# Last feed-forward network of a two-layer encoder: 18 of its 22 gate/up tile pairs as seven block products of 256 tokens, in place of eight

## What is computed

```python
D_MODEL, SEQ, D_FF = 1024, 512, 2816

def swiglu(h, w_gu, w_down):
    g, u = jnp.split(h @ w_gu, 2, axis=-1)
    return (jax.nn.silu(g) * u) @ w_down

# end of each layer i
h = modulate(rms_norm(x), sh3, sc3)
x = x + 0.5 * g3[:, None, :] * swiglu(h, ffn2_w_gu[i], ffn2_w_down[i])
x = rms_norm(x, post_gain[i])
```

## Time and profile before

| | before |
|---|---|
| median of 3 executions | 1981.63 us (1981.16 to 1982.28) |
| span of the profiled execution, first to last instruction | 1979.4 us |
| TensorE busy | 1951.1 us, 99% |
| VectorE busy | 1142.1 us, 58% |
| ScalarE busy | 720.1 us, 36% |
| GpSimd busy | 212.1 us, 11% |
| TensorE on the chain that ended last | 94% of the span |
| data moved by DMA | 263.97 MB, mean 133 GB/s |

### The profile page before, as it was taken

One profiled execution on the slowest core, in us unless ns is written; L12 is line 12 of the kernel. 1 busy time (PEld: TensorE's weight loads), 2 busy tenths in 40 slices (PEclk: granted clock), 3 DMA queues, 4 the chain that ended last, 5 costly groups with the idle time before them and its releaser, 6 DMA issues.

```text
span 1979.4 us, 23447 instructions
## 1 busy us (share of the span) xinstructions
PE 1951.1 (99%) x9060; PEld 1620.7 (82%) x9060; DVE 1142.1 (58%) x1720; ACT 720.1 (36%) x1068; POOL 212.1 (11%) x245
## 2 busy tenths in 40 slices
PE   6999999999999999999999999999999999999998
PEld 5888888888888888888888888878888888888887
DVE  7665564799857655645864453586554573333335
ACT  5222222464743213224422221356565452223134
POOL 3110000017701100100110000001101000000000
PEclk9999999999999999999999999999999999999999
DMA  8665552322126655622564443233322233222322
GB/s 336 227 215 172 197 191 96 106 89 86 33 64 223 204 185 183 235 81 89 172 200 138 165 155 116 91 101 113 96 86 86 62 103 106 103 88 94 97 80 69
DMA packets 76350, 263.97 MB, mean 133 GB/s; under 512 B 8897, under 2 KB 11073, under 8 KB 76274
## 3 DMA queue, kind: packets, MB, share of 16 engines
q1 hardware_dynamic: 55296, 190.34, 29.0%
q0 software_dynamic: 20256, 72.02, 11.1%
q10 hardware_dynamic: 722, 0.61, 0.1%
HBM read 260.66 MB, written 2.13 MB: 133 GB/s over the span
## 4 chain that ended last, share of the span: by engine, by line
PE 94%; DVE 3%; POOL 1%; issue 1%; DMA 0%; ACT 0%; SPq 0%; DVEq 0%; ACTq 0%; POOLq 0%
PE bank L1495 30%; PE bank L1500 29%; PE bank L1496 29%; PE bank L1943 1%; DVE dve_tmp L1068 1%; PE bank L1960 1%; PE bank L1875 1%; PE bank L1719 1%; DVE h_lo L1059 1%; PE bank L1721 1%; PE bank L1720 1%; PE bank L1932 0%; PE bank L1850 0%; DVE wlo L871 0%; POOL rstd L389 0%
## 5 line engine op out<-in xcount | busy, mean ns | idle before, releaser
L1495 PE MATMUL bank<-h_hi,whi 128*128 128x512 f32 x1808 | 711.3, 393 | 5.4 <-ACT h_hi L553 2.8
L1496 PE MATMUL bank<-h_hi,wlo 128*128 128x512 f32 x1808 | 705.1, 390 | 0.0
L1500 PE MATMUL bank<-h_lo,whi 128*128 128x512 f32 x1808 | 593.6, 390 | 2.4 <-POOL h_lo L405 2.4
L507 ACT ACTIVATE whi<-wraw 128x1024 fp32r<-128x1024 f32 x338 | 347.0, 1053 | 267.4 <-PE bank L1500 263.9
L871 DVE TENSOR_TENSOR wlo<-wraw,whi 128x1024 fp32r<-128x1024 f32 x324 | 388.9, 1223 | 60.1 <-ACT whi L507 59.8
L1495 PEld LDWEIGHTS bank<-h_hi,whi 128*128 128x128 f32 x1808 | 340.5, 188 | 78.9 <-issue 7.3
L1500 PEld LDWEIGHTS bank<-h_lo,whi 128*128 128x128 f32 x1808 | 339.7, 188 | 75.1 <-POOL h_lo L405 2.9
L1496 PEld LDWEIGHTS bank<-h_hi,wlo 128*128 128x128 f32 x1808 | 340.6, 188 | 68.7
L1495 PE MATMUL bank<-hid_hi,whi 128*128 128x512 f32 (+1 forms) x856 | 328.7, 384 | 0.0
L1500 PE MATMUL bank<-hid_lo,whi 128*128 128x512 f32 (+1 forms) x856 | 328.0, 383 | 0.0
L1496 PE MATMUL bank<-hid_hi,wlo 128*128 128x512 f32 (+1 forms) x856 | 327.9, 383 | 0.0
(11 more groups left out here) (256 smaller groups left out, 1359.5 us busy)
## 6 DMA issues: line engine op xcount, KB each, us to landing
wraw<-in_w_units_dram SPq DMA_DIRECT2D x306, 512.0 KB, 3.5
arena<-in_mod_t_dram POOLq DMA_DIRECT2D x96, 512.0 KB, 5.0
mod_tile<-in_mod_t_dram POOLq DMA_DIRECT2D x32, 512.0 KB, 4.9
wraw<-in_w_units_dram SPq DMA_DIRECT2D x32, 384.0 KB, 3.5
arena<-in_mod_t_dram SPq DMA_DIRECT2D x12, 512.0 KB, 9.6
arena<-in_w_units_dram SPq DMA_DIRECT2D x10, 512.0 KB, 4.5
xT<-in_xt_dram SPq DMA_DIRECT2D x8, 256.0 KB, 4.3
sq<-k_roots POOLq DMA_DIRECT2D x8, 256.0 KB, 3.6
```

The costliest lines, as they stand in the source:

```text
L507: act.activation(whi[:, s % RING, :, :], wraw[:, s % RING, :, :], ACT.Copy).then_inc(hi_ready, 1)
L1495: pe.matmul(dst, whi[:, w, k, :], hi_, start=first, stop=False)
L1496: pe.matmul(dst, wlo[:, w, k, :], hi_, start=False, stop=False)
L1500: return pe.matmul(dst, whi[:, s % RING, k, :], lo_, start=False, stop=last)
```

## The change

In FFN 3, pairs 4 to 7 of the first third and every pair of the other two are computed in another way (`SUM_PAIRS`, 18 pairs). The 128 x 1024 gate weights, the 128 x 1024 up weights and the 1024 x 512 input make a 2 x 2 by 2 x 2 block product: rows gate and up, K in halves `low_k` and `high_k`, tokens in halves `first` and `second`. Done block by block that is eight products (each of 4 K tiles, 128 rows, 256 tokens). The change does it with seven products of sums of blocks (the scheme of Strassen and Winograd) and adds the results. A block product is 12 matmuls of 256 tokens; a pair is 84 of them.

What that adds and moves:

- Once, before the first such pair, GpSimd makes `hsum = h_hi + h_lo` (8 instructions, `sum_h`) and four sums of its blocks of 128 x 1024 (`combine_h`). ACT rounds these (`round_t`) and DVE splits them (`split_t`). The fourth overwrites a part of `h_hi` and `h_lo`, so it waits for the last plain pair.
- For each such pair GpSimd makes four sums of weight blocks of 128 x 512 (`combine_w`).
- ACT and DVE split seven parts of 128 x 512 per pair (`part_hi`, `part_lo`) in place of two units of 128 x 1024. There is room in `whi` and `wlo` for the parts of one pair only, so part p of the next pair may be written when product p of this one is done (`part_free`).
- For each pair ACT copies two results of 256 tokens out of PSUM (`x_keep`, `z_keep`) and takes silu in two halves; DVE makes five sums of 256 tokens (`u2`, `u3`, two halves of `ups`, and the second half of `act_tmp`) and the product of 512, now with both inputs in SBUF. TensorE has a wait inside the pair ahead of five of the seven products.
- `hid_lo` of these pairs, "the remainder of the gated product", is made by GpSimd (`hid_rest`) and not by DVE.
- The buffers of the attention stage (`qk`, `pt_hi`, `pt_lo`, `v_hi`, `v_lo`) become slices of one tensor, `mix`, in which the split sums of `h` lie. The loops over pairs in FFN 3 are written out, not run as hardware loops. The name `job` now maps a unit to its number in the semaphore counts.

```diff
+SUM_FFN = (3,)
+PLAIN_PAIRS = 4
+SUM_PAIRS = [third_units(f, t)[0] + 2 * n for f in SUM_FFN for t in range(3)
+             for n in range(0 if t else PLAIN_PAIRS, THIRDS[t][1])]
+PRODUCTS = 7
...
+def part_free(s, p):
+
+    if s - 2 in SUM_PAIRS:
+        return job(s - 2) + p + 1
+    return job(s - RING + p // 2) + 1
...
+        MOVING_SUM = (0, 3, 1, 0, 2, 0, 4)
...
+            def combine_w(s, w):
+
+                n = SUM_PAIRS.index(s)
+                if n:
+                    pool.wait_ge(lo_ready, job(SUM_PAIRS[n - 1]) + (3, 2, 5, 6)[w])
+                g, u = s % RING, (s + 1) % RING
+                a11, a12, a21, a22 = wraw[:, g, low_k, :], wraw[:, g, high_k, :], wraw[:, u, low_k, :], wraw[:, u, high_k, :]
+                if w == 0:
+                    pool.wait_ge(raw_in[g], 16 * (s // RING + 1))
+                    pool.wait_ge(raw_in[u], 16 * ((s + 1) // RING + 1))
+                    pool.tensor_tensor(wcomb[:, 0, :, :], a21, a22, ALU.add).then_inc(w_combined, 1)
+                elif w == 1:
+                    pool.wait_ge(w_combined, 4 * n + 1)
+                    pool.tensor_tensor(wcomb[:, 1, :, :], wcomb[:, 0, :, :], a11, ALU.subtract).then_inc(w_combined, 1)
...
+            for t, (f0, k) in enumerate(THIRDS):
+                for tile in range(0 if t else PLAIN_PAIRS, k):
+                    s = third_units(3, t)[0] + 2 * tile
+                    if tile + 1 < k:
+                        for w in range(4):
+                            combine_w(s + 2, w)
+                    hid_rest(tile, HID_BASE[("ffn", 3)] + f0 + tile + 1)
+                if t < 2:
+                    for w in range(4):
+                        combine_w(third_units(3, t + 1)[0], w)
...
+            def sum_pair(s, tile):
+
+                n, j, q = SUM_PAIRS.index(s), job(s), tile % 2
+                x, _, z = sum_banks(s)
+                act.wait_ge(unit_done, j + 1)
+                act.wait_ge(evicted, s - 2)
+                act.activation(x_keep[q], x, ACT.Copy).then_inc(x_kept, 1)
+                next_hi(s, 0)
+                next_hi(s, 1)
+                act.wait_ge(unit_done, j + 3)
+                act.wait_ge(evicted, s)
+                act.activation(z_keep, z, ACT.Copy).then_inc(z_kept, 1)
+                next_hi(s, 2)
+                act.wait_ge(unit_done, j + 4)
+                act.activation(act_tmp[:, q, first], x, ACT.Silu)
+                next_hi(s, 3)
+                next_hi(s, 4)
+                act.wait_ge(c12_ready, n + 1)
+                act.activation(act_tmp[:, q, second], act_tmp[:, q, second], ACT.Silu).then_inc(act_out, 1)
+                next_hi(s, 5)
+                next_hi(s, 6)
+                act.wait_ge(evicted, s + 2)
+                act.activation(hid_hi[:, tile, :], dve_tmp[:, q, :], ACT.Copy).then_inc(hid_rounded, 1)
...
+                        if t == 0:
+                            up_body(up, 0, 0, True)
+                            up_body(up + 4, 0, 2)
+                            for m in range(4):
+                                round_t(m)
...
+            def sum_pair(s, tile, outs, rounded):
+
+                n, j, q = SUM_PAIRS.index(s), job(s), tile % 2
+                _, y, z = sum_banks(s)
+                next_lo(s, 0)
+                dve.wait_ge(x_kept, n + 1)
+                dve.wait_ge(unit_done, j + 2)
+                dve.tensor_tensor(u2, y, x_keep[q], ALU.add).then_inc(u2_ready, 1)
+                for p in (1, 2, 3):
+                    next_lo(s, p)
+                dve.wait_ge(unit_done, j + 5)
+                dve.tensor_tensor(u3, y, x_keep[q], ALU.add).then_inc(u3_ready, 1)
+                dve.wait_ge(z_kept, n + 1)
+                dve.wait_ge(u3_ready, n + 1)
+                dve.tensor_tensor(ups[:, second], u3, z_keep, ALU.add).then_inc(ups_ready, 1)
+                next_lo(s, 4)
+                dve.wait_ge(unit_done, j + 6)
+                dve.tensor_tensor(act_tmp[:, q, second], z, u2, ALU.add).then_inc(c12_ready, 1)
+                next_lo(s, 5)
+                dve.wait_ge(unit_done, j + 7)
+                dve.tensor_tensor(ups[:, first], y, x_keep[q], ALU.add).then_inc(ups_ready, 1)
+                dve.wait_ge(act_out, outs)
...
+                dve.tensor_tensor(dve_tmp[:, q, :], act_tmp[:, q, :], ups, ALU.mult).then_inc(evicted, 2)
+                next_lo(s, 6)
...
+            def sum_pair(s):
+
+                n, j = SUM_PAIRS.index(s), job(s)
+                x, y, z = sum_banks(s)
+                pe.wait_ge(evicted, s - 2)
+                for p, dst in enumerate((x, y, z, x, y, z, y)):
+                    if p == 3:
+                        pe.wait_ge(x_kept, n + 1)
+                    if p == 4:
+                        pe.wait_ge(u2_ready, n + 1)
+                    if p == 5:
+                        pe.wait_ge(z_kept, n + 1)
+                    if p == 6:
+                        pe.wait_ge(u3_ready, n + 1)
+                    if n == 0 and MOVING_SUM[p]:
+                        pe.wait_ge(t_split, MOVING_SUM[p])
+                    pe.wait_ge(lo_ready, j + p + 1)
```

More of the change, by code:

```diff
@@ L93, in down_tiles, with job, summed, part_of @@
     return range(first, first + 1)
+SUM_FFN = (3,)
[3 more added lines that the diff above has]
+PRODUCTS = 7
+def job(s):
+    return s + (PRODUCTS - 2) * sum(a < s for a in SUM_PAIRS)
+def summed(s):
+    return s in SUM_PAIRS or s - 1 in SUM_PAIRS
+def part_of(s, p):
+    return (third_start(s) + p // 2) % RING, 4 * (p % 2)
+def third_start(s):
+    return max(third_units(f, t)[0] for f in range(4) for t in range(3) if third_units(f, t)[0] <= s)
+def split_free(s):
+    if not summed(s - RING):
+        return job(s - RING) + 1
+    last = max(a for a in SUM_PAIRS if a < s)
+    return job(last) + min(2 * (s - last - 2) + 2, PRODUCTS)
+def part_free(s, p):
+    if s - 2 in SUM_PAIRS:
+        return job(s - 2) + p + 1
+    return job(s - RING + p // 2) + 1
+def raw_free(s):
+    a = s - RING
+    if not summed(a):
+        return job(a) + 1
+    return job(a) + PRODUCTS - 1 if a in SUM_PAIRS else job(a - 1) + PRODUCTS
 def dot_at(m):
@@ L483, in _, with sum_h, combine_h @@
                     fetch_bias(j + 1)
-            job(17, 4)
+            root_job(17, 4)
+            def sum_h():
+                for k in range(KT):
+                    pool.wait_ge(h_ready, KT * 5 + k + 1)
+                    pool.tensor_tensor(hsum[:, k, :], h_hi[:, k, :].bitcast(F32), h_lo[:, k, :].bitcast(F32), ALU.add)\
+                        .then_inc(h_summed, 1)
+            def combine_h(n):
+                h11, h12 = hsum[:, low_k, first], hsum[:, low_k, second]
+                h21, h22 = hsum[:, high_k, first], hsum[:, high_k, second]
+                dst, a, b = ((h11, h12, h11), (h12, h22, h12), (h22, h22, h11), (h21, h21, h22))[n]
+                pool.tensor_tensor(dst, a, b, ALU.subtract).then_inc(t_summed, 1)
@@ new lines, in _, with hid_rest @@
+            sum_h()
+            s0 = SUM_PAIRS[0]
+            pool.wait_ge(h_summed, KT)
+            combine_h(0)
+            combine_w(s0, 0)
+            combine_h(1)
+            pool.wait_ge(t_summed, 2)
+            combine_h(2)
+            combine_w(s0, 1)
+            pool.wait_ge(t_summed, 3)
+            combine_h(3)
+            combine_w(s0, 2)
+            combine_w(s0, 3)
+            def hid_rest(tile, rounded):
+                pool.wait_ge(hid_rounded, rounded)
+                pool.tensor_tensor(hid_lo[:, tile, :], dve_tmp[:, tile % 2, :], hid_hi[:, tile, :].bitcast(F32),
+                                   ALU.subtract).then_inc(hid_ready, 1)
@@ L1143, in ffn @@
                                 .then_inc(evicted, 2)
-                            if t < 2:
+                            if s + 4 in SUM_PAIRS:
+                                into = s + 4 if s + 2 not in SUM_PAIRS else s + 2
+                                for p in range(4) if into == s + 4 else range(4, PRODUCTS):
+                                    part_lo(into, p)
+                            elif t < 2:
                                 lo(s + 4)
@@ L1169, in ffn @@
                             add_x(down + d, d, 0, gate)
-                            lo(down + d + 4)
+                            if d < 4 or f not in SUM_FFN:
+                                lo(down + d + 4)
+                            else:
+                                for p in range(2 * d - 8, min(2 * d - 6, PRODUCTS)):
+                                    part_lo(down + KT, p)
                             for m in down_tiles(f, t, d):
```

169 lines of the change are left out of this document (140 added, 29 removed).

## The result

| | before | after |
|---|---|---|
| median of 4 executions | 1981.5 us (1981.2 to 1982.3) | 2032.6 us (2031.9 to 2033.3) |
| span of the profiled execution | 1979.4 us | 2031.5 us |
| TensorE busy | 1951.1 us, 99% | 1952.3 us, 96% |
| GpSimd busy | 212.1 us, 11% | 368.6 us, 18% |

The change makes the kernel slower: the ratio is 1.0257 (95% interval 1.0242 to 1.0271), +51.1 us. The forecast was 2024.6 us with a range to 2040.

The account below looks back on a forecast made before the run. TensorE's matmuls bound the kernel before; in changed pairs a circle through the other engines would. Pairs +27.7 (including the 14.4 gain), start +8.1, norm +4.5, down units +2.0, clock +1 give +43: 2024.6 us, range 1997 to 2040.

Parts of the forecast that it names:

- TensorE's own work: Matmuls of the 18 changed pairs: 10.08 us a pair for 10.88, saving 14.4 us.
- The circle: Dependences from one changed pair's `act_tmp` sum to the next, through DVE, ACT and GpSimd, not TensorE: 12.2 us without exclusion.
- Exclusion: GpSimd's and DVE's two-SBUF-input instructions keep each other out, 1.11 and 0.56 us; lengthens the circle from 12.2 to 13.6 us.
- the middle pair: Changed pairs of a third between its second and last: 13.6 us each.
- the second pairs: Second changed pair of each third, in which the circle starts: 13.1 us.
- the rival of whole instructions: Changed pairs: holds last the full 1.29 and 0.69 us, middle pair 14.6, total about +62 us; chance 0.09.
- The norm: Norm before the changed pairs: GpSimd's additions for `hsum` delay DVE's chain, so TensorE waits, +4.5 us.
- The start: Before the first changed pair's second product: wait for split sums of `h`, 6.0 us, +8.1 with GpSimd's weight sums.
- The clock: After the wait at the start of the changed pairs: TensorE may run at half pace for 2 to 4 us, +1 us.
- Down units: Down units wait for the last tile's remainder, now GpSimd's: 0.2 us in thirds of 8 tiles, 1.5 in the last; +2.0.
- without exclusion: Changed pairs: circle alone, 12.2 us a pair, about +17 us in all; chance 0.21 including weak exclusion.
- faster: Changed pairs: circle closes in under 10.08 us, TensorE runs through, -8 us in all; chance 0.05.

Follow-up runs that it names:

- e3: Changed kernel with the remainder made by DVE again and GpSimd's weight sums left out for all changed pairs but the first; output partly wrong; 1983.2 us.
- e6: Changed kernel with the four weight sums and the remainder made by DVE, its list reordered, the start left as changed; 1982.5 us.
- e7: e6 with the sums of h at the start also made by DVE, behind earlier plain pairs; GpSimd does nothing in this network; 1970.0 us.
- e2: Changed kernel with GpSimd's order alone changed: its four sums for the pair after the next stand ahead of this pair's remainder; 2006.4 us.
- e4: e3 with GpSimd's four sums per pair made again, into a buffer nobody reads behind the first pair; 2002.0 us.
- e9: e4 with each GpSimd instruction behind the first changed pair turned into a one-input copy of the same size; 1983.7 us.
- e5: Changed kernel with each of GpSimd's eight sums of h waiting for the whole norm, not its own K tile; 2035.0 us.

## Why the prediction was right

**TensorE's own work** was exact: 0.12 us from matmul to matmul, 10.06 us a pair in e3, e6 and e7. e7 cashes 11.9 of the 14.4 us.

**The circle**: right in its path and its size. Followed in the rows of after from `act_tmp`'s sum to the next (from 1691.97 to 1705.94) it takes 13.97 us for 13.6, with the stretches of the forecast at 0.45, 0.97, 1.96, 0.71, 4.45, 3.37 and 2.06 us, where it had 0.46, 0.99, 1.80, 0.69, 3.94 + 0.4, 2.31 + 1.0 and 2.02. e2, which changes only an order on it, shows that it binds.

**Exclusion**: right, and shown by e4 against e3, with e9 beside them. The holds were sized well: 1.16 us by a GpSimd instruction for 1.11, and 0.46 by one of DVE's (1.75 less 1.29) for 0.56. The 0.36 us by which the middle pair stood over 13.6 are spread over the circle; the largest parts are the 0.16 around the product, ahead of which DVE stood idle for 0.20 us for its own `ups`, and 0.11 in GpSimd's sums. With the second pairs, which took 13.4 for 13.1, this is 3.8 us of the 8. The measured pair, 14.0 us, lies between the forecast and the rival of whole instructions (14.6), but no hold in the rows is the whole 1.29.

**The norm**: 5.7 for 4.5 us, of the same cause, as e5 shows. Six of DVE's instructions were held up by 0.98 to 1.14 us and one, which fell behind two steps with an input in PSUM, by 0.05: 6.6 us, where the forecast had 5 to 6. The 1.55 us to spare taken off leaves 5.0; the 0.25 us that TensorE loses after each of its waits, four of them on `h_lo`, were not in the forecast.

**The start**: 8.25 for 8.1 us. Its two parts hold by themselves: two of DVE's instructions lost 1.06 us each, and in e3, where no GpSimd sum falls into this stretch, the wait with its restart is 6.0 us, the forecast's 6.0.

**The clock**: 2.8 for 1 us. That it might fall once, behind this wait, was right; mis-sized was the stretch, 6 us and not the 2 to 4 assumed.

**Down units**: 2.6 for 2.0 us, 0.4 in each of the first two thirds for 0.2, and 1.8 in the last for 1.5. The remainder was late at the last third as forecast (0.9 us, with 0.3 for its `hid_hi`), and TensorE's restart and the tail add to it.

**The rivals**: "without exclusion" is refuted by e4; "faster" needed a circle under 10.08 us, and e7 shows that the seven products can have it, though not with a GpSimd instruction of 0.7 us, as I had thought, but by leaving GpSimd out. I had summed DVE's load to 7.6 us and so had seen its 2.5 us of room. By the 0.69 us of a row the four sums and the remainder would not have fitted there (3.5); by the 0.60 from start to start all 18 instructions make 9.6 us, and they fit.

**Slips in the sums.** None changes the choice. The pairs of the rival without exclusion, summed as the forecast is, give +10.6 us over the three thirds and not +8.1, so some +19 in all. The +42 and +18 given with the exclusion leave the clock's 1 us out. The +62 of whole instructions has no working: nine middle pairs at 14.6 alone add 9 to the 43. The 4.5 for the norm is the upper end of 5 to 6 less 1.55, and 6.0 + 2 x 1.11 for the start is 8.2.

**The number**: every term of the table came out too small, by 8 us together and with nothing to set against it; the measured +51 lies within the +30 to +55 of the case that was forecast because that band was wide.
